# Expert stage in 32-slot blocks that gather and scatter for themselves, weights in a ring of nine 16 KB units

## The chip, the cores and the metric

The kernel runs on one core of one Trainium2 chip. The metric is the device time of the whole program in microseconds (us). It is given as the median of three runs.

## The reference

Two layers (DEPTH = 2) over 256 tokens of width 2048, all in float32. Each layer runs four token mixers off one input projection and one output projection, adds the result to `alpha * h` and normalises (layer norm). Then comes a mixture of experts, again with residual and layer norm. Cut to what matters here:

```python
def hier_moe(x, w_rg, b_rg, w_re, b_re, w_gate, w_up, w_down):
    g_prob = softmax(xt @ w_rg + b_rg)                  # 4 groups, the best one
    e_logits = (xt @ w_re + b_re).reshape(-1, 4, 4)     # 4 experts in each
    e_val, e_loc = lax.top_k(e_in_group, 2)             # the best two of that group
    e_w = softmax(e_val) * g_val
    combine = sum(one_hot(e_idx, 16) * e_w)
    for e in range(16):
        h = silu(xt @ w_gate[e]) * (xt @ w_up[e])       # 2048 -> 512
        out = out + combine[:, e:e + 1] * (h @ w_down[e])   # 512 -> 2048
    return out
```

Each of the 256 tokens goes to two experts, so a layer has 512 (token, expert) pairs, called slots. Counted from the reference with its inputs, the slots of the 16 experts are 32 25 19 30 20 23 25 38 38 38 41 39 36 25 36 47 in layer 0 and 29 30 23 38 28 32 24 30 26 35 34 27 36 33 46 41 in layer 1. An expert's weights are three matrices of 4 MB, 12.6 million bytes, and all 16 are read in each layer.

## The kernel before, in words

Every engine has one program with its own order, written out by hand, and they meet at semaphores. A layer has these parts.

**Mixers.** `project` (PE, line 687 on) multiplies the layer's input by 11 segments of 512 columns of `w_in`, then by 4 of `w_out`. The weights come in quarters of 1 MB into `w_raw` (6 places, `UNITS`). ACT rounds each to `w_hi` (`round_w`, L433), DVE writes the rest to `w_lo` (`split_w`, L964), and PE makes three products (L705, L843). Between the segments stand the mixers' own small matmuls. GpSimd (POOL) applies the layer norm's gain and offset to `h` (`affine`, L410 and L413, four operations of 128x2048), at the layer's start with `gb_in`, as soon as those vectors are loaded. In layer 0 the parameters are transposed (L674) and copied by DVE ahead of the first normalisation, and DVE computes a softplus in some 25 small operations (L1032 to L1057) between the first `split_w`.

**Route.** `turn` (L667) transposes the normalised `h`, PE computes the router's logits (L856, L862), and DVE picks group and experts in a chain of some 60 small operations (L1255 to L1326). It ends with the one-hot matrix `hot` of 512 slots, sorted by expert. The table `tabi` holds for each expert its first slot, its number of blocks and its first block.

**Gather.** PE multiplies `h` by `hot` for all 512 slots at once (L881: 16 chunks of 128 features, two token halves). ACT and DVE apply gain and offset on the way out of PSUM (L620, L967) to `xgT`. After it POOL runs `affine(gb)` on `h`.

**Expert stage.** A loop over 16 experts, and in it one over the expert's blocks of up to 64 slots (`expert_block`). PE in this order: gate and up projection in two halves (L900, 32 matmuls of 64 x 512, in two column tiles of the array), two transposes (L909), down projection (L917, 16 matmuls), eight transposes of the result (L926). DVE copies the block's columns (L1348, `xe`) and multiplies gate by up (L964). ACT does silu (L630), and the copies L632, L635 and L642, the last of which puts the block into `yT`. At the end of an expert's last block `release()` (a drain of PE, then `half_used`) frees each half of a matrix.

The weights lie in `ring`: three places of 32 KB per partition, one for gate, one for up, one for down, each loaded in two halves. SP issues the loads: `load_down(0)`, then gate and up of expert 0 as the output projection frees the places, and from expert 1 on each half when `half_used` says that its place is free. So 12.6 million bytes are loaded ahead of the first block.

**Scatter.** PE transposes `yT` (L945, 64 transposes), ACT and DVE copy it to `ySort`, and PE multiplies the weighted one-hot `pw` by it (L954, 32 matmuls of 512 columns). DVE adds the result to `ALPHA * h` (L1365), with the statistics (L1367). Then `normalize` (L977 to L967) and `turn` of the next layer, whose `round_w` and `split_w` follow.

A float32 matmul that is no transpose has two records in the trace (two passes), a transpose one.

Of the kernel before, what the change touches and what calls it, by code (L numbers as in the profile page):

```python
# [10 lines left out]
ALU = mybir.AluOpType  # L11
ACT = mybir.ActivationFunctionType
AX = mybir.AxisListType

P = 128
BLK = 64
KB = 256
SLOTS = 3
# [28 lines left out]
def trunk(nc, x, ln0_g, ln0_b, w_in, conv_a_w, conv_a_b, lru_wa, lru_ba, lru_wx, lru_bx, lru_lam, conv_b_w,  # L47
# [12 lines left out]
    S = 2 * T  # L60
    SP_ = S + BLK
# [5 lines left out]
    PER_E = 6 * E  # L67
# [6 lines left out]
    with ctx:  # L74
# [9 lines left out]
        def next_address():  # L84
            return (nc.sbuf_base + 31) // 32 * 32

        ring_at = next_address()
        ring = sb("ring", [P, SLOTS, KD * 512])
        h = sb("h", [P, NT, D])
        arena_at = next_address()  # L90
        arena = sb("arena", [P, 88 * KB])

# [4 lines left out]
        def area(kib, words):  # L97
            return arena[:, kib * KB:kib * KB + words]
# [4 lines left out]
        def late(kib, words):  # L103

            return ring[:, 2, kib * KB:kib * KB + words]
# [37 lines left out]
        hT_r = area(0, KD * T).rearrange("p (k t) -> p k t", k=KD)  # L143
        xgT = area(0, KD * SP_).rearrange("p (k s) -> p k s", k=KD)
        yT = area(36, KD * SP_).rearrange("p (k s) -> p k s", k=KD)
        ySort = area(0, 4 * D).rearrange("p (b n) -> p b n", b=4)
        hot = area(36, 2 * S).rearrange("p (t s) -> p t s", t=NT)
        hotw = area(40, 2 * S).rearrange("p (t s) -> p t s", t=NT)
        lgp = area(44, T)
        gb = area(52, 2 * D).rearrange("p (m n) -> p m n", m=2)  # L150
        xe = area(72, KD * BLK).rearrange("p (k s) -> p k s", k=KD)
        wr = area(78, KD * 32).rearrange("p (k n) -> p k n", k=KD)
        hmid, sgate = area(76, 256), area(77, 256)
        pw = area(78, 4 * T).rearrange("p (b t) -> p b t", b=4)
        hmT = area(82, 2 * P).rearrange("p (q n) -> p q n", q=2)
        yraw = area(83, 1024)
# [11 lines left out]
        slot_iota = sb("slot_iota", [P, S], mybir.dt.int16)  # L168
# [7 lines left out]
        def small(at, shape):  # L176
            n = int(np.prod(shape))
            ap = arena[:, 48 * KB + at:48 * KB + at + n]
# [10 lines left out]
        M = small(192, (3, NT, 16))  # L189
        pos, pos12 = small(320, (NT, 16)), small(352, (2, NT, 1))  # L190
        tab = small(384, (3, 16))
        scn = small(448, (2, 16))
# [10 lines left out]
        def w_raw(i):  # L203
            return ring_flat[:, i * 2048:i * 2048 + 2048].rearrange("p (k n) -> p k n", k=4)
# [1198 lines left out]
```

## Time and profile before

| | |
|---|---|
| median of 3 runs | 1976.12 us (1970.1 to 1976.12) |
| the profiled execution: its own time | 1975.3 us |
| its span | 1973.2 us |
| PE busy | 1681.7 us (85%) |
| DVE / ACT / POOL busy | 609.8 / 509.5 / 87.2 us |
| HBM read | 544.04 MB, 277 GB/s over the span |
| chain that ended last | PE 55%, DMA 24% |

The page first gives each engine's busy time, then the span in 40 slices with the clock granted to PE and the DMA rate, then the chain of work that ended last, followed back from the end, and then the costliest groups of instructions with the idle time ahead of them and what ended it. PE is the tensor engine's matmul, PEld its weight load, SP the engine that issues the loads. The timeline gives start and length of each piece in us. All of the sum is made against the profiled execution, whose own time lies 0.8 us under the median of the runs.

### The profile page before, as it was taken

The page shows a single profiled execution, that of the slowest core. Times are in us where ns is not written, and L with a number is a line of the kernel's source. Part 1 is how long each engine was busy: PE and PEld are TensorE (multiplying, and loading weights), DVE is VectorE, ACT ScalarE, POOL GpSimd, SP SyncE. Part 2 cuts the span into 40 slices and gives each one's busy share as a digit, 9 for nine tenths or more (in the row PEclk, how much of TensorE's full clock was granted, in tenths as well). Part 3 has the DMA queues.
Part 4 walks back from the last instruction along what each step waited for, and adds up shares of the span by engine and source line. Part 5 has one row for each costly group of instructions (what it writes and reads, how often), then busy time and mean ns, then how long its engine had stood idle before and what let it go on. Part 6 is the DMA issues. An engine that isn't in the chain of part 4 may idle for free.

```text
span 1973.2 us, 22680 instructions
## 1 busy us (share of the span) xinstructions
PE 1681.7 (85%) x9061; PEld 1086.5 (55%) x9062; DVE 609.8 (31%) x714; ACT 509.5 (26%) x562; POOL 87.2 (4%) x39
## 2 busy tenths in 40 slices
PE   5899999968878788787869999999688777887885
PEld 5799899854322223232468999988433222222332
DVE  7745645542000000000386464564510000000005
ACT  4343444311111111111234543432111111111120
POOL 4100000003000000000040000000030000000000
PEclk9899999989999999999979999999799999999998
DMA  8354455650999999999514544558249999999961
GB/s 289 134 170 140 147 169 181 242 226 22 426 428 425 425 427 426 425 427 400 180 64 171 175 144 141 176 191 312 93 170 426 426 426 427 425 426 428 426 290 43
DMA packets 119302, 547.06 MB, mean 277 GB/s; under 512 B 19940, under 2 KB 23240, under 8 KB 84680
## 3 DMA queue, kind: packets, MB, share of 16 engines
q1 hardware_dynamic: 117600, 546.02, 69.6%
q8 instruction: 48, 0.79, 0.2%
q10 hardware_dynamic: 1640, 0.13, 0.1%
q14 instruction: 14, 0.11, 0.0%
HBM read 544.04 MB, written 2.10 MB: 277 GB/s over the span
## 4 chain that ended last, share of the span: by engine, by line
PE 55%; DMA 24%; PEldq 5%; DVE 5%; issue 5%; PEld 2%; ACT 2%; DVEq 1%; SPq 0%; ACTq 0%
DMA ring<-in_w_up_dram 24%; PE ps L705 20%; PE ps L843 9%; PE ps L900 6%; PEldq L681 5%; PE ps L702 4%; PE ps L917 4%; PE ps L881 3%; PE ps L954 3%; PEld ps L900 2%; DVE w_lo L964 1%; DVE hT_lo L964 1%; PE ps L945 1%; PE ps L667 1%; DVE arena L964 1%
## 5 line engine op out<-in xcount | busy, mean ns | idle before, releaser
L900 PE MATMUL ps<-ring,arena 128*64 128x512 f32 x2048 | 482.0, 625 | 99.0 <-DMA ring<-in_w_up_dram 75.5
L900 PEld LDWEIGHTS ps<-ring,arena 128*64 128x64 f32 x2048 | 175.5, 143 | 384.9 <-issue 384.9
L964 DVE TENSOR_TENSOR w_lo<-ring,w_hi 128x2048 fp32r<-128x2048 f32 x120 | 283.9, 2378 | 260.1 <-ACT w_hi L433 259.6
L705 PE MATMUL ps<-hT_hi,w_hi 128*128 128x256 f32 x1152 | 333.4, 289 | 25.1 <-DVE w_lo L964 24.6
L705 PE MATMUL ps<-hT_hi,w_lo 128*128 128x256 f32 x1152 | 330.0, 286 | 0.0
L705 PE MATMUL ps<-hT_lo,w_hi 128*128 128x256 f32 x1152 | 329.7, 286 | 0.0
L433 ACT ACTIVATE w_hi<-ring 128x2048 fp32r<-128x2048 f32 x120 | 228.0, 1914 | 250.0 <-PE ps L705 133.4
L964 DVE TENSOR_TENSOR arena<-arena,ps 128x256 f32<-128x256 f32 (+1 forms) x34 | 15.9, 468 | 793.4 <-ACT arena L630 793.2
L705 PEld LDWEIGHTS ps<-hT_hi,w_hi 128*128 128x128 f32 x1152 | 225.3, 196 | 28.7 <-issue 17.9
L917 PE MATMUL ps<-ring,arena 128*64 128x512 f32 x1024 | 226.8, 595 | 15.1 <-ACT arena L632 15.1
L705 PEld LDWEIGHTS ps<-hT_hi,w_lo 128*128 128x128 f32 x1152 | 225.3, 196 | 0.7 <-issue 0.5
L705 PEld LDWEIGHTS ps<-hT_lo,w_hi 128*128 128x128 f32 x1152 | 225.2, 195 | 0.0
L917 PEld LDWEIGHTS ps<-ring,arena 128*64 128x64 f32 x1024 | 70.8, 137 | 150.5 <-issue 127.8
L630 ACT ACTIVATE arena<-ps 128x256 f32<-128x256 f32 x32 | 12.3, 384 | 454.8 <-PE ps L900 454.8
L843 PE MATMUL ps<-w_hi,mix_hi 128*128 128x512 f32 x256 | 99.6, 389 | 0.0
L843 PE MATMUL ps<-w_lo,mix_hi 128*128 128x512 f32 x256 | 99.6, 389 | 0.0
L843 PE MATMUL ps<-w_hi,mix_lo 128*128 128x512 f32 x256 | 99.6, 389 | 0.0
L635 ACT ACTIVATE arena<-ps 128x1024 f32<-128x1024 f32 x32 | 32.8, 1024 | 230.0 <-PE ps L917 230.0
L881 PE MATMUL ps<-arena,h 128*128 128x512 f32 x128 | 59.6, 629 | 11.5 <-DVE arena L1326 11.5
L926 PE MATMUL ps<-ident,arena 128*128 128x128 f32 x256 | 35.0, 279 | 36.0 <-ACT arena L635 36.0
L926 PEld LDWEIGHTS ps<-ident,arena 128*128 128x128 f32 x256 | 27.4, 140 | 64.1 <-ACT arena L635 64.1
L954 PE MATMUL ps<-arena 128*128 128x512 f32 x128 | 55.4, 593 | 1.7 <-ACT arena L647 1.7
(216 smaller groups left out, 1346.3 us busy)
## 6 DMA issues: line engine op xcount, KB each, us to landing
ring<-in_w_down_dram SPq DMA_DIRECT2D x64, 2048.0 KB, 18.3
ring<-in_w_gate_dram SPq DMA_DIRECT2D x64, 2048.0 KB, 16.3
ring<-in_w_up_dram SPq DMA_DIRECT2D x64, 2048.0 KB, 20.7
ring<-in_w_in_dram SPq DMA_DIRECT2D x88, 1024.0 KB, 4.8
ring<-in_w_out_dram SPq DMA_DIRECT2D x32, 1024.0 KB, 5.1
ring<-in_ln_g_dram SPq DMA_DIRECT2D x3, 1024.0 KB, 5.9
ring<-in_ln_b_dram SPq DMA_DIRECT2D x3, 1024.0 KB, 6.9
h<-in_x_dram SPq DMA_DIRECT2D x2, 1024.0 KB, 6.2
```

The source lines that it names most:

```text
L433: eng.activation(w_hi[n % 4][:], w_raw(n % UNITS), ACT.Copy).then_inc(w_rounded.sem, 1)
L635: eng.activation(yraw, banks(2, 2), ACT.Copy).then_inc(yraw_ready, 1)
L681: eng.drain().then_inc(half_used, 2)
L702: last = eng.matmul(ps[:, b + o, :], x_[:, kk, o * P:o * P + P], w_, start=opens, stop=ends)
L705: last = eng.matmul(ps[:, b + o // 2, (o % 2) * T:(o % 2) * T + T], w_[:, o * P:o * P + P], x_[:, kk, :], start=opens and o % 2 == 0, stop ...
L843: last = eng.matmul(ps[:, b + t, :], m[:, k, t * P:t * P + P], w, start=(q == 0 and k == 0 and j == 0), stop=(q == 3 and k == 3 and j == 2))
L881: last = eng.matmul(ps[:, k % 8, :], h[:, t, k:D:KD], hot[:, t, :], start=(t == 0), stop=(t == NT - 1))
L900: last = eng.matmul(ps[64 * c:64 * c + BLK, 0, :], xe[:, k, :], ring[:, 0:2, k * 512 + c * 256:k * 512 + c * 256 + 256], start=(k == 0), s ...
L917: last = eng.matmul(ps[r0:r0 + BLK, 2 + ch // 2, :], hmT[:, f % 2, 64 * (f // 2):64 * (f // 2) + BLK], slab_down(2)[:, f, ch * 512:ch * 51 ...
L926: last = eng.transpose(banks(4, 2)[:, q * P:q * P + P], yraw[:, q * P:q * P + P], ident[:])
L954: last = eng.matmul(ps[:, 2 * c + t, :], pw[:, sbk, t * P:t * P + P], ySort[:, sbk, c * 512:c * 512 + 512], start=(sbk == 0), stop=(sbk == 3))
L964: return eng.tensor_tensor(o, a, b, op)
```

## The change

Blocks have 32 slots (`BLK = 32`). From the slot counts above, layer 0 then has 24 blocks (experts 7 to 12, 14 and 15 have two, the others one) and layer 1 has 23 (experts 3, 9, 10 and 12 to 15 have two). Before, every expert had one block of 64.

A block gathers its own rows (`gather`, `turn_rows`) and scatters its own result (`scatter`): PE multiplies `hot` (32 columns for each token half, remade by DVE for each block in `mark`) by `h`, for the *next* block, between gate/up and down. The result of the *previous* block is scattered ahead of the down projection, into PSUM banks 4 to 7, and DVE adds each bank to `acc` (`add_block`), eight additions of 128x512 for a block. `acc` is a copy of `h`. The loop over experts is written out on PE, and ACT and DVE loop over blocks. `h` gets gain and offset before the gather, two of the four operations of 128x2048 by POOL with one by DVE between them and a third by POOL.

The weights lie in nine units of 16 KB per partition, 2 MB each: four units of gate and up together and two of down for an expert. Some lie where the mixers' buffers were. Units 0 to 8 are loaded ahead of the first block, and unit u waits until unit u - 9 has been used.

Beside this: `affine(gb_in)` waits until the ninth quarter of the layer is used. The parameters' transpose, its copy and the softplus move behind later quarters. `x` is loaded in four pieces.

The core of the diff:

```diff
-                def load_halves(e, m, w, i):
-                    eng.dma_start(slab(m)[:, 8 * i:8 * i + 8, :], src[:, 8 * i:8 * i + 8, :]).then_inc(slab_loaded[m][i], 16)
...
+                for u in range(PER_E * E):
+                    e, i = u // PER_E, u % PER_E
+                    if u >= SLOTS:
+                        eng.wait_ge(units_used, PER_E * E * l + u - SLOTS + 1)
...
+                    if i < 4:
+                        for m, w in enumerate((w_gate, w_up)):
+                            src = w[l, e].rearrange("(p k) n -> p k n", k=KD)
+                            eng.dma_start(unit_gu(u)[:, m], src[:, 4 * i:4 * i + 4, :]).then_inc(unit_loaded[u % SLOTS], 16)
...
                 eng.wait_ge(gb_in_loaded, 32 * (l + 1))
+                eng.wait_ge(w_used.sem, w_used.at(l, 9))
                 affine(gb_in)
...
+                def gather(count):
+                    eng.wait_ge(hot_ready, count)
                     for t in range(NT):
+                        for c in range(4):
+                            r0 = BLK * c
+                            last = eng.matmul(ps[r0:r0 + BLK, 3, :], hot[:, t, :],
+                                              h[:, t, :].rearrange("a (p k) -> a k p", k=KD)[:, 4 * c:4 * c + 4, :],
+                                              start=(t == 0), stop=(t == NT - 1), tile_position=(0, r0))
+                    last.then_inc(xrow_done, 1)
+                def turn_rows(count):
+                    eng.wait_ge(xrow_ready, count)
+                    for q in range(4):
+                        last = eng.transpose(ps[:, 3, q * P:q * P + P], xrow[:, q * P:q * P + P], ident[:])
+                    last.then_inc(xT_done, 1)
+                def scatter(g):
+                    eng.wait_ge(place_ready, g + l + 1)
+                    eng.wait_ge(y_ready, g + 1)
                     for t in range(NT):
+                        for c in range(4):
+                            r0 = BLK * c
+                            eng.wait_ge(added, (g + l) * 8 + 4 * t + c + 13)
+                            eng.matmul(ps[:, 4 + c, :], place[r0:r0 + BLK, t * P:t * P + P], yraw[r0:r0 + BLK, :],
+                                       start=True, stop=True, tile_position=(r0, 0)).then_inc(sc_done, 1)
 
                 def expert_block(g, e, last_block):
...
+                    for i in range(4):
+                        u = PER_E * e + i
+                        loaded(u)
+                        for k in range(4):
+                            x0 = (4 * k + i) * BLK
+                            for c in range(4):
+                                r0 = BLK * c
+                                last = eng.matmul(ps[r0:r0 + BLK, 0, 0:2 * P], xe[:, x0:x0 + BLK],
+                                                  unit_gu(u)[:, :, k, c * P:c * P + P],
+                                                  start=(i == 0 and k == 0), stop=(i == 3 and k == 3), tile_position=(0, r0))
...
+                        if last_block and i % 2:
                             release()
+                    gather(g + 2 * l + 2)
                     eng.wait_ge(hm_ready, g + 1)
+                    eng.transpose(ps[:, 1, 0:P], hmid, ident[:]).then_inc(hmT_done, 1)
+                    turn_rows(g + l + 2)
+                    scatter(g)
                     eng.wait_ge(hmT_ready, g + 1)
                     for f in range(KF):
...
+                        for c in range(4):
+                            r0 = BLK * c
+                            last = eng.matmul(ps[r0:r0 + BLK, 2, :], hmT[:, BLK * f:BLK * f + BLK],
+                                              unit_down(u)[:, f % 2, c * 512:c * 512 + 512],
+                                              start=(f == 0), stop=(f == KF - 1), tile_position=(0, r0))
                     last.then_inc(y_done, 1)
...
+                def add_block(g):
+                    for t in range(NT):
+                        for c in range(4):
+                            eng.wait_ge(sc_done, (g + l) * 8 + 4 * t + c + 1)
+                            sl = acc[:, t, c * 512:c * 512 + 512]
+                            tt(sl, sl, ps[:, 4 + c, :], ALU.add).then_inc(added, 1)
...
+                with eng.Fori(0, nb) as j:
+                    g = g0 + j
+                    eng.wait_ge(sg_ready, g + 1)
+                    tt(hmid, sgate, ps[:, 0, P:2 * P], ALU.mult).then_inc(hm_ready, 1)
+                    add_block(g)
+                    eng.scalar_tensor_tensor(place, rows[:, 0, :], slot_col, rows[:, 2, :], ALU.is_equal, ALU.mult)
+                    eng.scalar_tensor_tensor(place_2, rows[:, 1, :], slot_col, rows[:, 3, :], ALU.is_equal, ALU.mult)
+                    eng.drain()
+                    tt(place, place, place_2, ALU.add).then_inc(place_ready, 1)
+                    ts(slot_col, slot_col, float(BLK), None, ALU.add)
+                    mark()
```

**PE in one block.** The rows are PE's instructions of an expert's last block, `room` being the buffer that holds the weights and the work areas. Before (`ring` is the weights, `arena` the work areas):

```order
L900 MATMUL ps<-ring,arena 64x512 [waits slab_loaded_10,slab_loaded_00]
L900 MATMUL ps<-ring,arena 64x512 x15
L900 MATMUL ps<-ring,arena 64x512 [waits slab_loaded_11,slab_loaded_01]
L900 MATMUL ps<-ring,arena 64x512 x15
L909 MATMUL ps<-ident,arena 128x128 [waits hm_ready]
L909 MATMUL ps<-ident,arena 128x128
L917 MATMUL ps<-ring,arena 64x512 [waits slab_loaded_20,hmT_ready]
L917 MATMUL ps<-ring,arena 64x512 x7
L917 MATMUL ps<-ring,arena 64x512 [waits slab_loaded_21]
L917 MATMUL ps<-ring,arena 64x512 x7
L926 MATMUL ps<-ident,arena 128x128 [waits y_evac,yraw_ready]
L926 MATMUL ps<-ident,arena 128x128 x7
```

Now, from the fourth unit of gate and up (the three ahead of it have the same 16 matmuls):

```order
L908 MATMUL ps<-room 32x256 x15
L869 REGISTER_ALU
L873 MATMUL ps<-h,room 32x512 [waits hot_ready]
L873 MATMUL ps<-h,room 32x512 x7
L917 MATMUL ps<-ident,room 128x128 [waits hm_ready]
L881 MATMUL ps<-ident,room 128x128 [waits xrow_ready]
L881 MATMUL ps<-ident,room 128x128 x3
L891 ISA [waits y_ready,place_ready]
L892 MATMUL ps<-room 128x512 [waits added]
...
L927 MATMUL ps<-room 32x512 [waits unit_loaded_1,hmT_ready]
L927 MATMUL ps<-room 32x512 x7
```

Between gate/up and down now stand the next block's gather (L873), its transposes (L881) and the scatter of the block before (L892, eight times, each with its wait for `added`). The eight transposes at the block's end are gone.

**DVE in one block.** The loop body, before:

```order
L1348 ISA [waits gath_act,gu_done]
L1348 TENSOR_SCALAR arena<-arena 128x1024
L964 TENSOR_TENSOR arena<-arena,ps 128x256 [waits sg_ready]
L1345 REGISTER_ALU
L1345 COMPARE_AND_BRANCH
```

Now, with the eight additions in the middle, of which two are shown:

```order
L960 TENSOR_TENSOR room<-room,ps 128x128 [waits sg_ready]
L1355 ISA
L960 TENSOR_TENSOR room<-room,ps 128x512 [waits sc_done]
L1355 REGISTER_ALU
...
L1373 SCALAR_TENSOR_TENSOR room<-room 128x256
L1374 SCALAR_TENSOR_TENSOR room<-room 128x256
L960 TENSOR_TENSOR room<-room 128x256
L963 TENSOR_SCALAR room<-room 128x1
L963 TENSOR_SCALAR room<-room 128x32 x2
L1345 SCALAR_TENSOR_TENSOR room<-room 128x32 x2
```

DVE had two operations in a block and has eighteen.

## Rows read from the trace of the kernel before

**Rows 1.** Stretches of both expert stages: busy time by engine, clock, DMA share, GB/s.

```profile
core 0: us, PE busy (x) PEld busy (x) DVE busy (x) ACT busy (x) POOL busy (x), PEclk, DMA share, GB/s
489.00:930.00 441.00, 358.66 (x1605) 132.74 (x1605) 16.72 (x30) 62.44 (x90) 4.78 (x2) 0.97 1.01 424
1458.00:1900.00 442.00, 356.32 (x1608) 132.10 (x1606) 16.73 (x30) 62.45 (x90) 5.46 (x2) 0.97 1.00 424
```

**Rows 2.** Timeline of PE, the first block of layer 0: start, length.

```profile
480.51 8.66 PE L900 MATMUL ps<-ring,arena 128*64 128x512 f32 x32 [3.40 <-DVE arena L1348]
489.41 7.09 PE L900 MATMUL ps<-ring,arena 128*64 128x512 f32 x32 [0.23 <-issue]
497.43 0.44 PE L909 MATMUL ps<-ident,arena 128*128 128x128 f32 x2 [0.93 <-DVE arena L964]
498.33 7.09 PE L917 MATMUL ps<-ring,arena 128*64 128x512 f32 x32 [0.47 <-ACT arena L632]
```

**Rows 3.** Timeline of PE, the last block of layer 0 and what follows.

```profile
926.14 8.78 PE L900 MATMUL ps<-ring,arena 128*64 128x512 f32 x32 [2.71 <-DMA ring<-in_w_up_dram]
936.76 7.09 PE L917 MATMUL ps<-ring,arena 128*64 128x512 f32 x32 [0.47 <-ACT arena L632]
957.13 27.70 PE L954 MATMUL ps<-arena 128*128 128x512 f32 x64 [0.83 <-ACT arena L647]
990.20 6.40 PE L667 MATMUL ps<-ident,h 128*128 128x128 f32 x32 [5.37 <-DVE h L967]
```

**Rows 4.** Timeline of PE, the route and the gather of layer 0.

```profile
419.91 6.53 PE L667 MATMUL ps<-ident,h 128*128 128x128 f32 x32 [5.38 <-DVE h L967]
445.12 29.94 PE L881 MATMUL ps<-arena,h 128*128 128x512 f32 x64 [5.75 <-DVE arena L1326]
```

**Rows 5.** Timeline of PE, first and last block of layer 1.

```profile
1450.20 8.51 PE L900 MATMUL ps<-ring,arena 128*64 128x512 f32 x32 [3.39 <-DVE arena L1348]
...
1906.16 7.09 PE L917 MATMUL ps<-ring,arena 128*64 128x512 f32 x32 [0.47 <-ACT arena L632]
```

**Rows 6.** Timeline of PE, matmuls in four column tiles of 32, in layer 0's mixers.

```profile
51.92 1.93 PE L714 MATMUL ps<-ring,arena 128*32 128x256 f32 x32
```

**Rows 7.** Groups by shape, weight loads: busy us, mean ns of one.

```profile
L881 PEld LDWEIGHTS ps<-arena,h 128*128 128x128 f32 x128 | 37.9, 298 | 32.0 <-DVE arena L1326 11.7 <-issue 4.9
L954 PEld LDWEIGHTS ps<-arena 128*128 128x128 f32 x128 | 24.2, 190 | 31.7 <-issue 29.7 <-ACT arena L647 2.1
```

**Rows 8.** Groups by shape, operations of DVE, ACT and POOL alone.

```profile
L1365 DVE SCALAR_TENSOR_TENSOR h<-h,ps 128x512 f32<-128x512 f32 x16 | 11.0, 687 | 31.7 <-PE ps L954 31.7
L1104 DVE SCALAR_TENSOR_TENSOR ring<-arena,par,ring 128x255 f32<-128x255 f32 x8 | 3.3, 478 | 0.2
L647 ACT ACTIVATE arena<-ps 128x512 f32<-128x512 f32 x16 | 9.6, 598 | 8.7 <-PE ps L945 8.7
L410 POOL TENSOR_TENSOR h<-h,arena 128x2048 f32<-128x2048 f32 x4 | 18.8, 4732 | 844.6 <-PE ps L881 844.6
```

**Rows 9.** The chain that ended last, between two blocks: start, length, what.

```profile
561.26 0.11 PEld ps L926
...
562.45 0.22 PEldq L931
563.01 0.23 PEld ps L900 x4
```

**Rows 10.** Timeline of DVE and POOL at the entry of layer 1, and PE's wait there.

```profile
999.71 10.00 DVE L964 TENSOR_TENSOR hT_lo<-ring,hT_hi 128x1024 fp32r<-128x1024 f32 x2
997.58 11.04 POOL L410 TENSOR_TENSOR h<-h,ring 128x2048 f32<-128x2048 f32 x2
PE ps L705 <- DVE w_lo L964: 13.8, 1, 13.8
```

**Rows 11.** PE's clock in two short stretches of layer 0's expert stage.

```profile
927.00:931.00 4.00, 4.00 (x14) 1.51 (x12) 0.00 (x0) 0.00 (x0) 0.00 (x0) 0.57 1.01 422
505.00:509.00 4.00, 1.51 (x10) 0.85 (x8) 0.00 (x0) 2.11 (x3) 0.00 (x0) 1.00 1.02 438
```

More of the change, by code:

```diff
@@ L270, in expert_row @@
         def expert_row(eng, row, e):
-            hi = {0: S, 1: T // BLK, 2: 4096}[row]
-            return eng.value_load(tabi[0:1, row, bass.ds(e, 1)], min_val=1 if row == 1 else 0, max_val=hi)
+            lo, hi = {0: (1, T // BLK), 1: (0, 4096), 2: (1, NB_MAX)}[row]
+            return eng.value_load(tabi[0:1, row, bass.ds(e, 1)], min_val=lo, max_val=hi)
         def bank_order(head):
             return (head % 2) * 2 + head // 2
-        def block_start(first, j):
-            return nc.s_assert_within(first + j * BLK, 0, S, skip_runtime_bounds_check_because=
-                                      "a block starts at or before its expert's last slot")
@@ L645, in _, with copy_of @@
-                for c in range(0, 16, 2):
-                    eng.wait_ge(yS_done.sem, yS_done.at(l, c + 1))
-                    eng.activation(ySort[:, c // 4, (c % 4) * 512:(c % 4) * 512 + 512], ps[:, c % 8, :], ACT.Copy
-                                   ).then_inc(yS_act.sem, 1)
+                def copy_of(done, count, dst, b, ready):
+                    eng.wait_ge(done, count)
+                    eng.activation(dst, ps[:, b, 0:dst.shape[1]], ACT.Copy).then_inc(ready, 1)
+                eng.wait_ge(tab_ready.sem, tab_ready.at(l, 1))
@@ L922, in expert_block @@
                         release()
[L923 to L930 removed]
+                eng.wait_ge(tab_ready.sem, tab_ready.at(l, 1))
@@ new lines, in _ @@
+                g0, nb = expert_row(eng, 1, 0), expert_row(eng, 2, 0)
+                eng.wait_ge(h_ready, (2 * l + 2) * NT)
+                gather(g0 + 2 * l + 1)
+                for i in range(2):
+                    for j, col in ((0, pos12), (1, wts)):
+                        for t in range(NT):
+                            last = eng.matmul(banks(4, 2)[:, (2 * j + i) * T + t * P:(2 * j + i) * T + t * P + P],
+                                              col[:, i, t, :].to_broadcast([P, P]), ident[:], start=True, stop=True)
@@ L957, in _ @@
+                    expert_block(g1 + n - 1, e, True)
+                scatter(g0 + nb)
                 if l + 1 < L:
@@ new lines, in _, with mark @@
+                tt(carry[:], carry[:], tab[:, 2, 0:1], ALU.add)
+                eng.drain()
+                def mark():
+                    for t in range(NT):
+                        ts(hot[:, t, :], block_iota, pos12[:, 0, t, :], None, ALU.is_equal)
+                    eng.drain()
+                    for t in range(NT):
+                        last = eng.scalar_tensor_tensor(hot[:, t, :], block_iota, pos12[:, 1, t, :], hot[:, t, :],
+                                                        ALU.is_equal, ALU.add)
+                    last.then_inc(hot_ready, 1)
+                    eng.drain()
+                    ts(block_iota, block_iota, float(BLK), None, ALU.add)
```

500 lines of the change are left out of this document (216 added, 284 removed).

## The prediction

> **What bounds the kernel now.** The page's slices come first: through the two expert stages the DMA row stands at full. The windows put numbers to it: 441 us of a stage with a DMA share of 1.01 and 424 GB/s, while PE is busy for 359 us [rows 1]. An expert's 12.58 MB take 29.7 us at that rate. PE's own block is three times 7.09 us, two transposes, eight more and their gaps, some 27 us [rows 2], so PE waits for a load in each expert [rows 3]. Around the stage PE or a chain through it sets the pace. From the end of the turn (419.91 + 6.53 = 426.4) to the first block (480.51) pass 54.1 us, 30 of them the gather [rows 4, 2]. From the first block to the end of the last down projection pass 943.85 - 480.51 = 463.3 us, in layer 1 1913.25 - 1450.20 = 463.1 [rows 2, 3, 5]. From there to the next turn pass 990.20 - 943.85 = 46.3 us, 27.7 of them the scatter's product [rows 3]. At the entry of a layer PE waits 13.8 us for DVE, which takes 10.0 us for two operations that took 1.23 each before POOL began; POOL's two took 11.04 [rows 10].
>
> **The new block on PE.** Gate/up: 64 matmuls of 256 columns, 128 records, in four column tiles. Thirty-two such records took 1.93 us [rows 6], the first 0.22, so 0.055 each: 7.0 us. Gather: 16 records of 512 columns. In two tiles a record takes 7.09 / 32 = 0.222 us [rows 2], so in four 0.111: 1.8 us. Its moving operand is `h` with features 64 bytes apart. As stationary operand that layout took 298 ns a load against 190 [rows 7]; less the 84 ns at which the closely packed loads run that is 214 against 106, twice. I double: 3.6 us. The ends are 1.9 (the layout costs a moving operand nothing) and 7.0 (strided and only two tiles overlap). Transposes with the copy between (0.6 us, the ACT row of rows 8): 1.3 us. Scatter: four matmuls, then four more of which each waits for DVE's addition into the same bank, 0.69 us each [rows 8]; 1.2 for the first product, eight additions less those that start early: 5.1 us. The ends are 4.3 and 6.4. Down: 32 records of 0.111 = 3.6 us. Between blocks 1.8 us where PE drains and reads the table, as now (561.26 to 563.01 [rows 9]), otherwise 0.2. Sum: 7.0 + 3.6 + 1.3 + 5.1 + 3.6 + 1.8, with two drains inside gate/up of 0.23 each [rows 2], = 22.9 us for an expert's last block, 20.8 for one that another follows (less 1.6 at its end and 0.5 of drains). An expert with one block stays under the 29.7 us of its weights. One with two takes 43.7 and does not.
>
> DVE's eighteen operations are eight of 0.69, three of up to 0.48 and small ones, about 8.3 us in a block [rows 8]: hidden.
>
> **The stage.** The nine units are there at the start; the first is released after a cold quarter, at about 7.2 us, and a unit of 2.1 MB takes 4.95 us, so unit u lands at 7.2 + (u - 8) x 4.95. Experts of one block run at the loads' pace. In layer 0 the first expert with two is number 7: its unit 45 lands at 190.4, gate/up ends at 192.3, the block at 206.1, its second at 229.0. From here PE is always late: experts 8 to 12 give 5 x 43.7, 13 gives 22.9, 14 and 15 87.4; less the last turn of 1.8 this is 556.0 us. Before: 463.3. **+92.7.** In layer 1 doubles stand at 3, 9, 10 and 12 to 15; what expert 3 loses, the ring catches up. Unit 57 lands at 249.7, gate/up ends at 251.6, expert 9 at 288.3, 10 at 332.0, 11 at 354.9, the last four at 529.7, less 1.8: 527.9 against 463.1. **+64.8.** So 17 + 13 = 30 blocks run at PE's pace, and each microsecond of a block is worth 30 in all. That is why the sum is so uncertain.
>
> **What goes.** Ahead of the stage the gather of 29.94 us becomes one block's own, some 3.8, and transposes. But `h` now has to have gain and offset first: POOL's operations of 4.7 us [rows 8] run beside the router's chain on DVE, as POOL's did in rows 10, and the one-hot comes about 9 us later. I put the first gate/up at 463, 36.5 us after the turn: -17.6. Behind the last block 46.3 becomes a copy of 0.6, eight matmuls with additions (8.3), eight statistics of 0.69 that no longer lie between the additions (5.5) and the normalisation (3.5), less rounding 17.3 with its gaps: -29.0. Twice both: **-93.2.**
>
> **The entries.** `affine(gb_in)` waits for the ninth quarter, so the 13.8 us wait [rows 10] should go, with the slow clock behind it some 16. But POOL's 20 us come all the same, and then slow `split_w` when it has a lead of some quarters. I take -11 for each layer, between 0 (the wait only moves) and -16. The parameters' transposes off the start give another -2.8. **-24.8.** The softplus counts in that 11 for layer 0. `x` in four pieces changes only how early the first statistics start: nothing.
>
> **Sum:** 92.7 + 64.8 - 93.2 - 24.8 = +39.5. On the profiled execution's 1975.3 us that gives 2014.8; the runs' median is 0.8 above it. I predict **2015**.
>
> **Two rules against the trace.** Rows 6 show 32 records in four tiles in 1.93 us, so 0.055 each, which is a quarter of a lone record's 0.22: full overlap, for 256 columns and one shape. The Trainium skill ("TensorE: Matmul & The Clock Gate", Measured speedup vs the span model) has four row tiles at 3.07 times and three column tiles at 2.38 times one. By that, gate/up, gather and down would take some 4.3 us more in a block, and the sum would be near 2144. It is part of the second rival.
>
> The strided `h` is priced by rows 7, two to one. The Trainium skill ("SBUF — State Buffer", Specifications (TRN2), on lines of 16 bytes) says that an access pattern that doesn't use a line twice in a row loses rate; by that the doubling holds for the moving operand too, and no row of before shows it there.
>
> **Rival 1, the block is shorter, and the change wins.** PE still sets the doubles' pace but the gather's stride is free (1.9), the scatter's additions start early (4.3), transposes take 1.1 and the turn 1.2. Last block 19.5, other 17.9, pair 37.4. By the same steps layer 0 gives 192.3 + 10.9 + 19.5 = 222.7, then 187 + 19.5 + 74.8 - 1.2 = 502.8 (+39.5), layer 1 487.3 (+24.2). With -93.2 and -24.8: -54.3, 1921 us. It decides from a block 39.5 / 30 = 1.3 us shorter than mine on. For it: each of those ends is a row of before's trace without a penalty. Against it: rows 7, and rows 9, where the turn takes 1.8. Chance 0.30.
>
> **Rival 2, the block is longer.** In the stretch of transposes and scatter PE is mostly idle, for over 6 us in each block. Before, the clock stood at 0.57 over 927 to 931 behind a wait of 2.71 us and a part of 7.09 took 8.78 [rows 3, 11]; yet after the gaps of a block's middle it stood at 1.00 [rows 11]. If it falls once in each block: 1.7 x 30 = +51, 2066. If the gather's tiles overlap only by twos: +3.4 x 30 = +102, 2117. If all four-tile work overlaps by three, 4.3 x 30 = +129, 2144. Middle 2100, chance 0.20. That the four tiles don't overlap at all here, so that the change doesn't do what it says, is the end of this case and needs rows 6 to be an exception; I give it no chance of its own.
>
> **How the numbers follow.** My own case has 0.50 and reaches from 1965 to 2060 by its entries and the scatter's bounds; a tenth of it lies below the time before. A difference of 0.3%, 6 us, is about what a measurement can tell. Faster: 0.30 from rival 1 and 0.04 from my case; same 0.05; slower 0.41 from my case and 0.20 from rival 2: 0.61. The range takes rival 1 but for its tail (entries at -16 and a tail shorter still) and half of rival 2: 1905 to 2115.
>
> **What would show it.** PE's timeline of a block: gate/up in 7.0, gather 3.6, the eight matmuls of the scatter over about 5, down 3.6, the turn 1.8. The DMA row must fall below full in the slices of the experts with two blocks, from 190 us after the first block on, and the chain there must run through PE and DVE's additions. First block near 463, last down to next turn 17 us, no wait of 13.8 for `w_lo` at the entry. I am wrong if the pair of blocks takes under 40 us, if the clock falls within blocks, or if the loads are still the end of the chain in the last experts.

## The result and the profile after

The changed kernel takes 2145.8 us (median of 4 runs, 2135.88 to 2152.52) where the kernel before takes 1976.12: a ratio of 1.0848, with a 95% interval of 1.0785 to 1.0912. The direction was forecast, the size was not. 2015 was predicted, and the range ended at 2115. The profiled execution has a span of 2142.3 us against 1973.2, +169.1.

By PE's timeline that splits as follows. A stage runs from the first gate/up to the end of the last down projection.

| stretch, us | before | after | forecast change | measured change |
|---|---|---|---|---|
| to the turn of layer 0 | 419.9 | 412.2 | -13.8 | -7.7 |
| turn of layer 0 to first block | 54.1 | 38.5 | -17.6 | -15.6 |
| stage of layer 0 | 463.3 | 607.9 | +92.7 | +144.6 |
| last down to next turn | 46.3 | 15.9 | -29.0 | -30.4 |
| mixers of layer 1, turn to turn | 400.7 | 393.0 | -11.0 | -7.7 |
| turn of layer 1 to first block | 53.5 | 38.1 | -17.6 | -15.4 |
| stage of layer 1 | 463.0 | 594.4 | +64.8 | +131.4 |
| last down to the end | 60.0 | 29.3 | -29.0 | -30.7 |

(The forecast's -24.8 for the entries stands in rows 1 and 5 as 13.8 and 11.0.) Everything around the stages came within 2.3 us of its forecast, but for the entries, which gave 15.4 instead of 24.8. The stages cost 276 us more instead of 158. So the question is where 118 us of the stages come from.

The page of the changed kernel: the chain's shares, and the DMA queues.

```profile
PE 79%; issue 9%; DVE 8%; ACT 2%; DVEq 1%; DMA 1%; SPq 0%; ACTq 0%
...
q1 hardware_dynamic: 138496, 546.10, 66.1%
q8 instruction: 146, 2.39, 0.4%
```

DMA has gone from the chain (24% before) and PE has 79%, as forecast. But 9% of the chain are `issue`, time in which PE waits for nothing that the profile names. The queue that brings instructions moved 146 packets, where it moved 48 before. PE's waits name the place:

```profile
PE ps L908 <- issue: 156.5, 40, 8.6
PE ps L892 <- DVE room L960: 36.0, 49, 0.8
PE ps L881 <- ACT room L627: 21.2, 47, 0.5
```

The timeline of PE from the end of one block (L927, down) to the gate/up of the next (L908), columns as in [rows 2]. These are experts 0 to 2 of layer 0:

```profile
480.24 4.97 PE L927 MATMUL ps<-room 128*32 128x512 f32 x32
493.23 9.07 PE L908 MATMUL ps<-room 128*32 128x256 f32 x128 [8.03 <-issue]
502.58 3.62 PE L873 MATMUL ps<-h,room 128*32 128x512 f32 x16 [0.28 <-issue]
...
512.24 3.64 PE L927 MATMUL ps<-room 128*32 128x512 f32 x32
524.20 8.95 PE L908 MATMUL ps<-room 128*32 128x256 f32 x128 [8.32 <-issue]
```

And this is a full expert with two blocks, number 8, with the start of the next:

```profile
719.23 7.11 PE L908 MATMUL ps<-room 128*32 128x256 f32 x128 [1.93 <-issue]
726.13 3.64 PE L873 MATMUL ps<-h,room 128*32 128x512 f32 x16
729.70 0.33 PE L917 MATMUL ps<-ident,room 128*128 128x128 f32 x1
730.48 0.66 PE L881 MATMUL ps<-ident,room 128*128 128x128 f32 x4 [0.44 <-ACT room L627]
731.06 1.14 PE L892 MATMUL ps<-room 32*128 32x512 f32 x8
732.96 3.11 PE L892 MATMUL ps<-room 32*128 32x512 f32 x8 [0.76 <-DVE room L960]
736.00 5.09 PE L927 MATMUL ps<-room 128*32 128x512 f32 x32
740.91 7.41 PE L908 MATMUL ps<-room 128*32 128x256 f32 x128
...
758.25 3.64 PE L927 MATMUL ps<-room 128*32 128x512 f32 x32
...
763.89 7.11 PE L908 MATMUL ps<-room 128*32 128x256 f32 x128 [2.00 <-issue]
```

The pair is what was forecast: gate/up 7.1, gather 3.64, scatter 5, down 3.6 (5.1 where the clock is low), 44.66 us from 719.23 to 763.89 where the sum said 43.7. The single block is not. Its work is the same 23 us, but ahead of it stand 8 us instead of 1.9. The first expert of a layer aside, 1.9 to 2.1 us stand ahead of every expert with two blocks. Of the 15 with one, 11 have 7.6 to 8.6 us, and four have 2.2 to 2.3 and, after 2 to 24 records, a second stall of 4.2 to 4.9. In PE's program each expert has two bodies, one for blocks that another follows and one for the last. An expert with two blocks runs through both; one with a single block jumps over the first body. That gave the theory: **the jump leads to instructions that are not yet there.** The rival was a load or an `xe` that comes late without the profile naming it.

Two windows of layer 0's stage, experts 0 to 5 and then mostly pairs, columns as in [rows 1]:

```profile
457.00:650.00 193.00, 135.08 (x1186) 50.92 (x1190) 43.95 (x108) 24.22 (x39) 0.00 (x0) 0.86 0.93 380
650.00:950.00 300.00, 263.39 (x2575) 106.66 (x2574) 95.42 (x234) 45.75 (x78) 0.00 (x0) 0.95 0.72 294
```

PE is idle for 30% of the first window, and the loads run at 380 GB/s and not at the 424 of [rows 1]: neither is at its limit.

### The profile page after: what moved, and what is told of

Its sections match the earlier page's. It is cut to its first block, busy times and chain, and to the rows that moved or that the text cites. A ratio compares the mean times of both kernels' runs of the same rounds, so it can differ in the third digit from the quotient of the medians.

```text
span 2142.3 us, 34368 instructions
## 1 busy us (share of the span) xinstructions
PE 1799.2 (84%) x14632; PEld 1127.9 (53%) x14632; DVE 911.3 (43%) x1469; ACT 529.8 (25%) x627; POOL 77.5 (4%) x38
## 4 chain that ended last, share of the span: by engine, by line
PE 79%; issue 9%; DVE 8%; ACT 2%; DVEq 1%; DMA 1%; SPq 0%; ACTq 0%
PE ps L695 18%; PE ps L908 18%; PE ps L927 10%; PE ps L892 9%; PE ps L873 8%; PE ps L837 8%; DVE room L960 3%; PE ps L692 3%; PE ps L881 1%; ACT room L627 1%; DVE w_lo L960 1%; DVE room L963 1%; PE ps L665 1%; DMA room<-in_w_in_dram 1%; DVE h L960 1%
## 5 line engine op out<-in xcount | busy, mean ns | idle before, releaser
L960 DVE TENSOR_TENSOR room<-room,ps 128x512 f32<-128x512 f32 (+2 forms) x445 | 257.8, 640 | 861.6 <-ACT room L642 592.7
L908 PE MATMUL ps<-room 128*32 128x256 f32 x6016 | 378.0, 406 | 159.9 <-issue 156.5
L908 PEld LDWEIGHTS ps<-room 128*32 128x32 f32 x6016 | 218.2, 117 | 336.0 <-issue 247.1
L960 DVE TENSOR_TENSOR w_lo<-room,w_hi 128x2048 fp32r<-128x2048 f32 x120 | 278.9, 2337 | 242.9 <-ACT w_hi L444 242.6
L444 ACT ACTIVATE w_hi<-room 128x2048 fp32r<-128x2048 f32 x120 | 228.7, 1915 | 242.1 <-PE ps L695 122.5
L627 ACT ACTIVATE room<-ps 128x512 f32<-128x512 f32 x192 | 94.5, 518 | 625.4 <-PE ps L927 407.5
L892 PE MATMUL ps<-room 32*128 32x512 f32 x784 | 207.2, 652 | 37.7 <-DVE room L960 36.0
L927 PE MATMUL ps<-room 128*32 128x512 f32 x1504 | 208.2, 704 | 0.0
L873 PE MATMUL ps<-h,room 128*32 128x512 f32 x784 | 177.5, 1031 | 17.6 <-issue 8.9
L892 PEld LDWEIGHTS ps<-room 32*128 32x128 f32 x784 | 74.5, 183 | 132.8 <-DVE room L960 121.4
L927 PEld LDWEIGHTS ps<-room 128*32 128x32 f32 x1504 | 50.4, 126 | 156.2 <-issue 156.2
L873 PEld LDWEIGHTS ps<-h,room 128*32 128x32 f32 x784 | 26.0, 119 | 102.6 <-issue 92.0
```

The source lines that it names most:

```text
L444: eng.activation(w_hi[n % 4][:], w_raw(n % UNITS), ACT.Copy).then_inc(w_rounded.sem, 1)
L627: eng.activation(dst, ps[:, b, 0:dst.shape[1]], ACT.Copy).then_inc(ready, 1)
L873: last = eng.matmul(ps[r0:r0 + BLK, 3, :], hot[:, t, :], h[:, t, :].rearrange("a (p k) -> a k p", k=KD)[:, 4 * c:4 * c + 4, :], start=(t = ...
L892: eng.matmul(ps[:, 4 + c, :], place[r0:r0 + BLK, t * P:t * P + P], yraw[r0:r0 + BLK, :], start=True, stop=True, tile_position=(r0, 0)).the ...
L908: last = eng.matmul(ps[r0:r0 + BLK, 0, 0:2 * P], xe[:, x0:x0 + BLK], unit_gu(u)[:, :, k, c * P:c * P + P], start=(i == 0 and k == 0), stop ...
L927: last = eng.matmul(ps[r0:r0 + BLK, 2, :], hmT[:, BLK * f:BLK * f + BLK], unit_down(u)[:, f % 2, c * 512:c * 512 + 512], start=(f == 0), s ...
```

## The experiments

**1. PE's program without the jumps.** The loop over experts was already written out. Here the blocks are too, for the routing of these inputs; all registers are still read.

```diff
-                    with eng.If(n > 1):
-                        with eng.Fori(0, n - 1) as j:
-                            expert_block(g1 + j, e, False)
+                    if e in ((7, 8, 9, 10, 11, 12, 14, 15), (3, 9, 10, 12, 13, 14, 15))[l]:
+                        expert_block(g1, e, False)
                     expert_block(g1 + n - 1, e, True)
```

> PE's program is written out block by block for these inputs (no If and no Fori around a block; the registers are still loaded), so no body of instructions is jumped over. Code-jump theory: the gap ahead of a single-block expert falls from about 8 us to the 2 us that stand ahead of a two-block expert; the single-block experts then run at the loads' pace of 29.7 us instead of 31, so layer 0's stage gets about 37 us shorter (608 to 571) and layer 1's about 59 (594 to 535), 2145 to about 2050. Rival, the 8 us are a wait for a late unit or for xe that the profile does not name: the gap and the time stay at 2145.

Measured: 2047.85 us (ratio to the kernel before 1.0348, interval 1.0308 to 1.0389). Stages 563.4 and 543.3 us, where 571 and 535 were expected. PE's timeline at expert 1, then at expert 6, where PE now waits for the loads, and its waits:

```profile
479.60 7.42 PE L908 MATMUL ps<-room 128*32 128x256 f32 x128 [1.71 <-issue]
...
609.19 3.66 PE L908 MATMUL ps<-room 128*32 128x256 f32 x64 [1.81 <-issue]
614.98 2.55 PE L908 MATMUL ps<-room 128*32 128x256 f32 x32 [2.13 <-DMA room<-in_w_up_dram]
```

```profile
PE ps L908 <- issue: 57.5, 32, 3.1
...
PE ps L908 <- DMA room<-in_w_up_dram: 27.7, 13, 4.6
```

The 8 us are 1.7, and the single-block experts run at the loads' pace (421 GB/s), as the prediction had assumed for the changed kernel. With gate/up right behind down its clock is high too: 7.42 instead of 9.07. This is 98 us of the 131 that were missing.

**2. The gather without its stride.** `h[:, t, 512 * c:512 * c + 512]` in place of the columns 64 bytes apart. It computes another order of features, so its output is not the reference's.

> The gather reads 512 neighbouring columns of h instead of every sixteenth, so its features are in another order and the output is another. Stride theory: the 16 records take 1.8 to 1.9 us instead of 3.62, and as PE sets the pace in every block, 49 gathers give -86 us, 2145 to about 2060. Rival, two of the four tiles overlap only (the second rival of the prediction): the 3.62 stay, 2145. If the loads were the bound of the single-block experts, only 30 gathers would count: about 2090.

Measured: 2068.95 us, -77.

```profile
495.70 1.92 PE L873 MATMUL ps<-h,room 128*32 128x512 f32 x16 [0.28 <-issue]
```

1.92 against 3.62: the stride costs 1.7 us in each gather, and the four tiles overlap fully (0.12 a record, where two tiles have 0.222 and the untiled product of [rows 3] has 27.70 / 64 = 0.43). The 77 us are most of the 83 that 49 gathers would give: no expert of this program is bound by its loads. With other values layer 1 also routes otherwise (its expert 5 has two blocks and its expert 10 one, still 23 in all). Layer 0, whose blocks are the same, has a stage of 573.9 us instead of 607.9, which is 1.4 for each of its 24.

**3. The kernel before with its loop written out.** `for e in range(E)` for `eng.Fori(0, E)` on PE, nothing else.

> The kernel before, with PE's loop over the experts written out and nothing else changed; every expert has one block, so in each a body is jumped over that is not in PE's instruction memory. Code-jump theory: a gap of up to 8 us between blocks instead of 1.8; PE's 27 us of a block become about 33 and pass the loads' 29.7, +3.5 x 32 = +112, 1976 to about 2088 (less if the shorter body of this block is fetched faster). Rival, writing the loop out costs nothing: 1976, gap 1.8.

Measured: 1986.95 us (ratio 1.0046, interval 1.003 to 1.0062): +10, not +112. PE's timeline at expert 1 of the kernel before, and at experts 1 and 2 here:

```profile
509.06 7.09 PE L900 MATMUL ps<-ring,arena 128*64 128x512 f32 x32 [1.43 <-issue]
```

```profile
509.56 7.09 PE L900 MATMUL ps<-ring,arena 128*64 128x512 f32 x32 [0.93 <-issue]
...
535.91 4.45 PE L900 MATMUL ps<-ring,arena 128*64 128x512 f32 x11 [0.79 <-issue]
541.85 4.88 PE L900 MATMUL ps<-ring,arena 128*64 128x512 f32 x21 [1.49 <-issue]
```

The turn between blocks is even shorter: 0.9 instead of 1.4 on the same timeline ([rows 9] count from the last weight load and have 1.8). Sometimes a stall of 0.4 to 2.3 us follows. Only 6 us of the difference lie in the two stages (466.2 us each). In the traces 7.5 lie in the mixers of layer 1, where PE's wait for `w_lo` is 17.7 us instead of 13.8, and why is open. Here too each expert's first body is jumped over, but it has 58 matmuls, not 101. So the theory as I had put it, a jump costs 6 us, was incomplete: what is passed over must be long enough. Runs 9 to 11 measure that.

**4. Without the wait for the ninth quarter.** `eng.wait_ge(w_used.sem, w_used.at(l, 9))` is taken out of the changed kernel.

> The changed kernel without the wait of affine(gb_in) for the ninth quarter. If the later start of POOL is what took 7.7 and 7.1 us off the two mixer parts, the 13.8 us wait of PE for w_lo at the entry of layer 1 comes back and the time rises by 10 to 20 us, 2145 to about 2160. Rival: the time POOL takes only moves, 2145 within 5.

Measured: 2143.62 us, no difference. The rival holds: POOL's time only moves. In layer 1 the mixers take 396.7 us without the wait and 393.0 with it; in layer 0 the turn comes at 408.3 without it and at 412.2 with it. (The other runs of the new stage, which all have the wait, lie at 391.5 to 394.5 and at 408.9 to 412.4, so the gain of layer 1 stands out, and the loss in layer 0 is between 0.6 and 4.) POOL's line in this run (entry of layer 1) shows why the old entry does not come back even without the wait:

```profile
1094.34 11.46 POOL L416 TENSOR_TENSOR h<-h,room 128x2048 f32<-128x2048 f32 x2 [5.15 <-DMA room<-in_ln_b_dram]
```

POOL starts 6.1 us after the turn (which ends at 1088.2), because `ln_b` lands later. In [rows 10] it started beside DVE's writes of `hT_lo`; here DVE ends those at 1094.8, so POOL's time falls on `split_w`, and PE's longest wait for `w_lo` in that stretch is 6.2 us instead of 13.8.

**5. One body for an expert.** The same for any routing: a single body in a loop over the expert's blocks, and a short `If` over each `release()`.

```diff
-                    with eng.If(n > 1):
-                        with eng.Fori(0, n - 1) as j:
-                            expert_block(g1 + j, e, False)
-                    expert_block(g1 + n - 1, e, True)
+                    with eng.Fori(0, n) as j:
+                        expert_block(g1 + j, e, j - n + 1)
...
-                        if last_block and i % 2:
-                            release()
+                        if i % 2:
+                            with eng.If(last_block > -1):
+                                release()
```

> PE's program has one body for each expert instead of two, in a loop over its blocks; the drains that free units are passed over by short jumps when another block follows. Works for any routing. Code-jump theory: the gap ahead of the 17 single-block experts falls from 8 us to about 2. For the 15 second blocks it jumps back over a whole body: if that costs the same 6 us as the jump forward, the time is e1_straight's 2048 + 90 = about 2138; if the body is still at hand, about 2050. Rival, each If and its registers is what cost the time: a stall at every release, above 2145.

Measured: 2069.46 us (ratio 1.0438). A second block and the next expert's first, on PE's timeline:

```profile
664.05 7.41 PE L908 MATMUL ps<-room 128*32 128x256 f32 x128
687.07 3.23 PE L908 MATMUL ps<-room 128*32 128x256 f32 x56 [2.04 <-issue]
```

The jump back over a whole body leaves no gap ahead of the second block, and the gaps ahead of single blocks are 2.0 to 2.1 us. The 22 us to run 1 are spread: turns longer by 0.3 in 32 experts are 10 of them, and the rest fits more parts at the low clock (0.90 granted over 700 to 850 us, where run 1 has 0.95).

**6. The gather without its stride, and right.** Run 1 with the columns of run 2, and gate and up loaded as `"(k p) n -> p k n"`, so that rows and features agree again.

> e1_straight with the gather reading 512 neighbouring columns of h, and gate and up loaded with their rows in the same order (a partition then gets pieces of 2 KB instead of 8 KB), so that the reference's output is computed. Stride theory: -1.7 us in each of the 30 blocks at PE's pace, 2048 to about 1997. Rival, the loads get slower with 2 KB pieces and the single-block experts lose it again: 2010 to 2040, with a DMA rate under 420 GB/s there.

Measured: 2019.87 us, -28, inside the rival's range (2010 to 2040) and with the rate that it asked for. The first window is among single-block experts of layer 0 in run 1, the second the same here:

```profile
560.00:650.00 90.00, 63.68 (x579) 23.59 (x575) 22.00 (x54) 10.56 (x18) 0.00 (x0) 0.91 1.01 421
```

```profile
560.00:650.00 90.00, 62.10 (x559) 23.71 (x559) 22.00 (x54) 10.56 (x18) 0.00 (x0) 0.85 1.04 398
```

Pieces of 2 KB instead of 8 KB bring 398 instead of 421 GB/s, and the loads bound these experts. What the pairs gain is partly lost there.

**7. The scatter in two halves.** Run 1 with the first four matmuls of the scatter ahead of the gather.

```diff
+                    scatter(g, (0,))
                     gather(g + 2 * l + 2)
                     eng.wait_ge(hm_ready, g + 1)
...
-                    scatter(g)
+                    scatter(g, (1,))
```

> e1_straight with the first four matmuls of the scatter moved ahead of the gather, so that DVE adds four banks while PE gathers. If the scatter's 4.8 us are DVE's pace, they become 1.14 + 1.14, -2.5 us in each of 30 blocks, 2048 to about 1973. Rival, the additions are slowed or come late beside the gather (place or y not ready so early): a wait ahead of the gather, 2048 or above.

Measured: 1952.59 us, ratio 0.9869 (0.9845 to 0.9893): 1.3% faster than the kernel before, and 20 us better than expected.

```profile
726.91 1.14 PE L892 MATMUL ps<-room 32*128 32x512 f32 x8
727.98 3.61 PE L873 MATMUL ps<-h,room 128*32 128x512 f32 x16
731.52 0.33 PE L918 MATMUL ps<-ident,room 128*128 128x128 f32 x1
732.31 0.66 PE L881 MATMUL ps<-ident,room 128*128 128x128 f32 x4 [0.46 <-ACT room L627]
732.89 1.14 PE L892 MATMUL ps<-room 32*128 32x512 f32 x8
733.97 3.64 PE L928 MATMUL ps<-room 128*32 128x512 f32 x32
```

Both halves take 1.14 and none waits for DVE: from 4.8 us to 2.3. A pair at the high clock takes 42.7 us in run 1 and 38.1 here, 2.3 a block, which for 30 blocks is 70 of the 95 us gained. The rest fits the clock: in run 1, 22 of the 47 down projections took 4.9 to 6.3 us instead of 3.64, and here none did. Why it no longer falls was not tried. Over 700 to 850 us run 1 is granted 0.95 and this one 1.00:

```profile
700.00:850.00 150.00, 137.50 (x1556) 57.10 (x1552) 57.12 (x138) 27.79 (x48) 0.00 (x0) 1.00 0.83 338
```

**8. Runs 6 and 7 together.**

> e6_rows and e7_split together: 2048 - 51 - 75 = about 1922, under the kernel before (1977). If PE's pace in pairs comes near the loads' 29.7 us, less is gained; a pair should take 44 - 3.4 - 5 = 35.6 us, still above. Rival: the clock falls more often when PE is less loaded and gives back 1.7 us a pair, about 1950.

Measured: 1934.18 us, ratio 0.9783 (0.9753 to 0.9812). The 1922 that was expected is missed by 12, by the slower loads and not by the clock that the rival named: no down projection took over 4.7 us. Against run 7 all of the stages' gain lies in layer 0 (499.8 against 513.2 us); layer 1 has 497.7 against 497.3. There, counted from the first gate/up, the slower loads bring expert 9's second block 13 us later than in run 7. Only 13 blocks (17 in layer 0) run at PE's pace and can make up for that, and expert 12 waits for its loads once more, 5.8 us.

**9 to 11. The jump alone.** Run 5 with a branch that is never taken into its body, ahead of each expert, over 48, 96 or 192 matmuls:

```diff
+                    with eng.If(n > 7):
+                        for m in range(96):
+                            eng.matmul(ps[0:BLK, 0, 0:2 * P], xe[:, 0:BLK], unit_gu(0)[:, :, 0, 0:P], start=True, stop=True)
                     with eng.Fori(0, n) as j:
```

> e5_one_body with a branch ahead of each expert over 48 matmuls that are never run (about the body of the kernel before). If only the fact of a jump out of what is at hand costs, the gap ahead of each expert is 8 us as in the changed kernel, and now for the two-block experts too: about 2069 + 32 x 6 less what the loads hide, some 2190. If the price grows with the length that is passed over, the gap is near 2 to 4 us: 2069 to 2100.

> The same with 96 matmuls, about one body of the changed kernel. Code-jump theory: the gap of 8 us comes back ahead of every expert, also of those with two blocks, 2145 plus up to 6 x 15, some 2190 to 2235. Rival, the 8 us came from something in the two-body program other than the jump: 2069.

> The same with 192 matmuls. If a miss has one price, as e11_jump96. If the instructions passed over are fetched all the same, about twice the gap: 14 us, and the time 2350 or more.

Measured: 2093.73, 2237.2 and 2327.68 us, against 2069.46 without the branch. With 48, PE's timeline has gaps of 2.4 and behind some of them a second stall of 0.3 to 4.2:

```profile
479.01 4.39 PE L908 MATMUL ps<-room 128*32 128x256 f32 x69 [2.44 <-issue]
484.21 3.64 PE L908 MATMUL ps<-room 128*32 128x256 f32 x59 [0.81 <-issue]
```

With 96 it is the picture of the changed kernel, ahead of both kinds of expert: 7.2 to 9.0 us in about half of them, 2.4 to 2.6 and a second stall of up to 5.1 in most others. This one, expert 8, has two blocks:

```profile
721.77 8.47 PE L908 MATMUL ps<-room 128*32 128x256 f32 x128 [8.31 <-issue]
```

With 192 a gap of 8 to 9 ahead of nearly all, and often a second one:

```profile
702.02 1.93 PE L908 MATMUL ps<-room 128*32 128x256 f32 x14 [8.69 <-issue]
707.42 9.05 PE L908 MATMUL ps<-room 128*32 128x256 f32 x113 [3.47 <-issue]
```

So the stall is the jump's, as 1 had shown by taking it away. 48 came out as the growing price had it (2069 to 2100), 96 as the theory had it (2190 to 2235, measured 2 above); 192 lies between its two expectations, above one price for every miss and below twice the gap. The queue of instructions moved 95 packets in run 5 (16.4 KB each by the page), and 119, 143 and 159 here: 24 more, 48 more, and then 64 instead of 96. By these counts the instructions that are passed over are fetched all the same up to 96 matmuls, and of the 192 a part is left out. The Trainium skill ("Runtime: NRT & Kernel Launch", Instruction fetch mechanics) says that instructions are fetched in sequence, in blocks of 16 KiB, and that a taken branch out of the pages at hand must wait for its target's; the packets' size and the gaps agree. It is not in proportion to what is passed over: +24, +168 and +258 us for 1, 2 and 4 parts. Between 48 and 96 matmuls it goes from small to some 6 us more than a turn. What stays open is the exact length where it sets in, and why a second stall follows at times.

The stall also depends on what the DMA engines do meanwhile. Ahead of the last expert of a layer all weights have landed. This is run 11 at layer 0's expert 14 and at its expert 15, first PE's timeline, then the DMA share inside the two gaps (columns as in [rows 1]):

```profile
1060.82 8.86 PE L908 MATMUL ps<-room 128*32 128x256 f32 x125 [8.24 <-issue]
1109.31 8.49 PE L908 MATMUL ps<-room 128*32 128x256 f32 x128 [5.53 <-issue]
```

```profile
1052.60:1060.80 8.20, 0.00 (x0) 0.01 (x1) 0.00 (x0) 1.88 (x2) 0.00 (x0) 0.80 1.02 422
1103.70:1109.20 5.50, 0.08 (x4) 0.00 (x0) 0.18 (x1) 1.88 (x2) 0.00 (x0) 0.96 0.01 3
```

In layer 1 the last gap is 5.5 us too. In run 10 that of layer 0's last expert is 5.7, and in layer 1 it is 2.5 with a second stall of 1.8. So some 3 of the 8 us go with the full weight loads beside them. That rests on four gaps; no run varied the loads alone.

**12. The best version for any routing.** Run 5 with the scatter of run 7 and the gather of run 6.

> e5_one_body (any routing) with the scatter in two halves around the gather and the gather of neighbouring columns with rows loaded to match. By the differences measured on e1_straight (-114 for both), 2069 - 114 = about 1955, between 1935 and 1970, faster than the kernel before by about 1%. Rival: a second block's jump back, hidden in e5 behind PE's slower pace, now shows, about 2000.

Measured: 1948.55 us in 6 runs, ratio 0.9849 (0.9826 to 0.9872). It computes the reference for any routing and is 1.5% faster than the kernel before.

## Why the prediction was wrong, point by point

**What bounds after.** Right: DMA left the chain, PE and DVE's additions form it. The rates fall below full already in the single-block experts, though, which was not expected.

**The block on PE.** Right in each term: gate/up 7.1 and 7.4 (7.0 and two drains), gather 3.62 (3.6), scatter 4.8 and 0.3 around it (5.1), down 3.64 (3.6), the turn 1.9 (1.8), a pair 44.66 in the one shown (43.7). The clock in the pairs is the exception: over both stages 20 of the 47 down projections took 4.8 to 6.3 us instead of 3.64. This window holds the end of the scatter and the first half of the down projection of the pair shown:

```profile
734.00:738.00 4.00, 4.00 (x19) 1.18 (x20) 3.93 (x9) 0.00 (x0) 0.00 (x0) 0.69 0.00 0
```

The price that had to be borrowed, twice the time for columns 64 bytes apart, is what run 2 measured: 3.62 against 1.92. The Trainium skill ("SBUF — State Buffer", Specifications (TRN2)) has the rule that an access must use a line of 16 bytes at least twice for the full rate, and run 2 agrees that less costs. The Trainium skill's 3.07 times for four row tiles ("TensorE: Matmul & The Clock Gate", Measured speedup vs the span model) is not what the column tiles of this kernel show: 128 records of 256 columns took 7.11 us, 0.055 each, a quarter of the 0.22 that the untiled product of [rows 3] gives for 256 columns. The sum of 2144 that I had drawn from that page is near the measured time, but by accident: none of its 4.3 us a block is there.

**The step that failed** is the sentence "An expert with one block stays under the 29.7 us of its weights", with "between blocks 1.8 us where PE drains and reads the table, as now". The 1.8 was read at [rows 9], in a kernel whose loop came back to the same instructions and whose jump passed over 58 matmuls. The change writes the loop out and makes the body 101 matmuls long. A single block then has 8 us ahead of it and, behind the pause, a gate/up that starts at the low clock (0.50 granted over 493.3 to 495.3 us) and takes 9.0 us instead of 7.4: 31 us, over its loads. Run 1 puts that at 98 us. I had named the written-out loop in the description of the change and given it no price. The Trainium skill has a sentence against the jump on the page named at runs 9 to 11, and it was not weighed. On the same page the Trainium skill prefers full unrolling to control at run time, and of the three forms the one without any branch (run 1) was indeed the fastest. The unrolled loop with a branch in it was the dear one, and the single body in a loop (run 5) cost 98 - 76 = 22 us more than no branch at all, against 98 for the two bodies.

**The rest of the 131 us.** The stages of run 1, free of the jumps, are 563.4 and 543.3 against the sum's 556.0 and 527.9: 22.8 us. Some 10 of them lie ahead of the blocks that PE bounds: the gate/up of expert 7 was put at 192.3 us after the first gate/up began and ended at 196.1, that of layer 1's expert 9 at 251.6 and ended at 257.9. The loads' 421 GB/s instead of 424 are 1 to 2 us of each; where the rest comes from is open. The other 12.7 lie in the pairs and the single expert between them. The clock falls in most pairs, behind the transposes and the scatter, and the following down takes 5.1 instead of 3.64. A pair then takes 44.4 us, and 42.7 where the clock stays high; the sum had 43.7. One pair, with two such stretches, took 49.4. Rival 2 had that mechanism, but once in each block. The entries account for another 9.4, and route and tail for 1.1.

**Route and tail** came within 2.3 us each, the tail with some luck: its terms of 0.6, 8.3, 5.5 and 3.5 add up to 17.9 and not to the 17.3 that was used, and 15.9 was measured.

**The entries** were taken at -24.8 and gave -15.4. By run 4 the deferral gives 3.7 us in layer 1 and loses about as much in layer 0, nothing in the whole time, and it was the reason given for -22 of them: a right sign with a wrong cause. How the 15.4 split between the parameters' transposes, the softplus and the later `ln_b` was not tried.

**Two slips in the working.** The 84 ns taken off the weight loads stand in no row. They are what the traces' loads of 32, 64 and 128 columns (110, 137 and 190 ns) leave for none, an extrapolation; without them the layout's price would have been 298 / 190, 1.6 times instead of the 1.9 that run 2 measured. Overlap by three instead of four would cost 14.2 / 3 = 4.7 us a block, not the 4.3 that goes with 3.07 times.

**The rivals.** Rival 1 asked for a block 1.3 us shorter; the blocks were not, and runs 2 and 7 show what it took to make them so. Rival 2 came nearer in its total, but by luck: tiles that overlap by twos or threes did not occur, the clock fell in 13 of the 30 blocks and not in each, and the jump stood in neither rival.

## What to carry to other kernels

A loop that is written out is paid for in instructions: a branch over a body of some hundred matmuls cost PE some 5 to 6 us each time and shows in the profile only as `issue` ahead of the first instruction behind it. Here it came to 98 us, where the whole change had been forecast at +39.5. Share one body in a loop; a jump back over the same body left no gap here. (To order the bodies so that the usual case jumps over nothing would be another way; it was not tried.) And where a product waits for DVE to empty its banks, put half of it ahead of other PE work: that alone gave 95 us, some 25 of them with the clock.

## What was not expected of the hardware

- A branch forward over 48 matmuls costs little (+24 us for 32 of them), over 96 some 5 us each (+168), over 192 some 8 (+258); the gap is about 8 us whether 96 or 192 are passed over. The jump back over a body of 101 showed no gap.
- The same gap was 5.5 to 5.7 us where the DMA engines stood idle (share 0.01) and 8 to 9 where they were full.
- Loads in pieces of 2 KB run at 398 GB/s where pieces of 8 KB run at 421, with the DMA share at full in both.
